# A decoder layer on one core: three more pairs of weight blocks computed with seven half products each

## The reference, cut to what matters

```python
h = x @ lw['w_in']
cq, ckv, kr, conv_in, ga, gb = jnp.split(h, IN_OFFSETS, axis=-1)
...
mix = (jax.nn.sigmoid(ga) * branch_a + jax.nn.sigmoid(gb) * branch_b) @ lw['w_out']
```

## Time and profile before

| | us |
|---|---|
| median of 3 runs (lowest to highest) | 949.93 (947.04 to 950.75) |
| the profiled execution | 949.91 |
| its span from first to last instruction | 948.2 |
| busy in the span: TensorE / VectorE / ScalarE / GpSimd | 908.6 / 466.2 / 247.4 / 96.8 |
| the chain that ended last: TensorE / DMA / VectorE | 77% / 13% / 6% |

### The profile page before, as it was taken

The page is one execution under the profiler, slowest core; times in us unless marked ns, Lnnn a source line. Parts: engine busy times, 40 slices in busy tenths (PEclk is TensorE's granted clock), DMA queues, the critical chain, the costliest instruction groups (busy, mean ns, idle before and its releaser), DMA issues.

```text
span 948.2 us, 14012 instructions
## 1 busy us (share of the span) xinstructions
PE 908.6 (96%) x5269; PEld 545.3 (58%) x5269; DVE 466.2 (49%) x1053; ACT 247.4 (26%) x540; POOL 96.8 (10%) x146
## 2 busy tenths in 40 slices
PE   8999999999999999999999999889999899897997
PEld 7777777777777766565668744443333333333444
DVE  2344477776634238777675545671111211013784
ACT  1122121122135015566640110221111111011336
POOL 0111211211211200000000000011211111111000
PEclk9999999999999999999999999999999999899999
DMA  9866898989797811011043297549999999998501
GB/s 377 351 244 244 317 331 285 306 312 344 272 357 260 288 40 54 28 40 42 10 183 153 86 429 310 203 134 394 421 424 423 423 424 424 424 417 351 229 24 66
DMA packets 65419, 247.53 MB, mean 261 GB/s; under 512 B 11301, under 2 KB 12078, under 8 KB 56358
## 3 DMA queue, kind: packets, MB, share of 16 engines
q1 hardware_dynamic: 46742, 191.41, 51.8%
q0 software_dynamic: 13216, 35.28, 10.2%
q10 hardware_dynamic: 5392, 19.93, 5.5%
HBM read 240.98 MB, written 18.05 MB: 273 GB/s over the span
## 4 chain that ended last, share of the span: by engine, by line
PE 77%; DMA 13%; DVE 6%; ACT 2%; issue 2%; SPq 1%; DVEq 0%; ACTq 0%; POOLq 0%
PE ps L1019 16%; DMA arena<-in_wexp 10%; PE ps L1512 9%; PE ps L1432 6%; PE ps L1356 4%; PE ps L1534 4%; PE ps L963 4%; PE ps L1107 3%; PE ps L1078 3%; PE ps L1192 3%; PE ps L1010 3%; PE ps L1637 2%; PE ps L1216 2%; PE ps L1156 2%; PE ps L1173 2%
## 5 line engine op out<-in xcount | busy, mean ns | idle before, releaser
L1019 PE MATMUL ps<-arena 128*128 128x260 f32 x736 | 170.7, 387 | 1.4 <-DMA arena<-in_xT 1.0
L1019 PEld LDWEIGHTS ps<-arena 128*128 128x128 f32 x736 | 137.5, 191 | 29.7 <-issue 7.5
L2043 DVE SCALAR_TENSOR_TENSOR arena<-arena,vec 128x512 f32<-128x512 f32 x120 | 81.8, 744 | 0.0
L2852 POOL DMA_DIRECT2D arena<-in_kv x96 | 51.7, 540 | 259.9 <-issue 255.4
L1512 PE MATMUL ps<-arena 128*64 128x512 f32 x288 | 66.0, 612 | 7.7 <-DMA arena<-in_wexp 6.6
L2677 DVE TENSOR_TENSOR arena<-ps,arena 128x256 f32<-128x256 f32 x18 | 7.6, 424 | 130.5 <-ACT arena L1893 130.5
L1512 PE MATMUL ps<-arena,con 128*64 128x512 f32 x288 | 65.6, 608 | 4.6 <-DMA arena<-in_wexp 4.6
L1534 PE MATMUL ps<-arena 128*64 128x512 f32 x288 | 66.8, 606 | 3.4 <-DMA arena<-in_wexp 3.4
L1432 PE MATMUL ps<-arena 128*128 128x512 f32 x128 | 58.0, 600 | 0.0
L1534 PEld LDWEIGHTS ps<-arena 128*64 128x64 f32 x288 | 21.8, 140 | 45.7 <-issue 45.7
L1512 PEld LDWEIGHTS ps<-arena 128*64 128x64 f32 x288 | 21.6, 141 | 45.9 <-issue 44.6
(11 more groups left out here) (402 smaller groups left out, 1292.6 us busy)
## 6 DMA issues: line engine op xcount, KB each, us to landing
arena<-in_wexp SPq DMA_DIRECT2D x26, 2048.0 KB, 27.1
arena<-in_kv SPq DMA_DIRECT2D x160, 272.0 KB, 9.1
arena<-in_wexp SPq DMA_DIRECT2D x36, 1024.0 KB, 27.2
arena<-in_kv POOLq DMA_DIRECT2D x96, 272.0 KB, 7.4
arena<-in_w ACTq DMA_DIRECT2D x35, 512.0 KB, 7.8
arena<-in_wexp SPq DMA_DIRECT2D x16, 512.0 KB, 9.0
arena<-in_wo SPq DMA_DIRECT2D x8, 512.0 KB, 4.2
arena<-in_w_out SPq DMA_DIRECT2D x4, 1024.0 KB, 7.4
```

Source lines behind the costliest of these rows:

```text
L1019: y = mm(ps[:, b + h, 0:TH], w[:, k], xT[:, k, h * TH:(h + 1) * TH], start=(k == 0), stop=(k == KD - 1))
L2043: y = v.scalar_tensor_tensor(out=aT[:, c, 0:NPR], in0=win, scalar=wt, in1=aT[:, c, 0:NPR], op0=ALU.mult, op1=ALU.add)
L2852: pool.dma_start(rec[:, n % 2, SPN + j], a["kv"][bass.ds(pg, 1)].rearrange("a p n -> (a p) n")).then_inc(s_kvp[n % 2], 16)
```

## The change

Gate blocks `gb` 2 to 7 (units 18 to 23) become three more pairs, numbers 3 to 5, with seven half products each. `gate_tokens` makes the token sums for them again, in the memory where `mix` is written later, since the convolution has by then overwritten the first ones; it stands in VectorE's program behind the last block of the convolution. The outputs of a pair, and the copy of `m1`, now go straight to their place in `hT` or `sigB` (`half_out`), without the scratch tiles `m1p` and `u2p`. The squares of the kv latent (`sqkv`) and the weight sums of pair 4 lie in gate blocks that are not yet written. The weight sums of pair 3 stand ahead of the reciprocal in unit `gb` 1. The sigmoid of gate blocks 0 to 3 waits for the last `c12` of pair 3, that of 4 to 7 for that of pair 5. The numbers of taps for each half unit change (`TAPS_LESS`), and since a pair counts 28 calls where two units counted 32, the places of some steps move: the program has 530 calls instead of 542, `k_step` 4 goes from unit `ks` into the second half of `gb` 0, `k_step` 5 to 7 lie behind the first half unit of pairs 3, 4 and 5, the turns behind their second and the `v_step`s behind their third; further on some steps move by one half unit. The banks' parity follows (`banks_of`, `paired_bank`).

The diff, cut:

```diff
...
-PAIRED = [5, 7, 9]
+AT = {u: i for i, u in enumerate(UNITS)}
+GROUPS = [5, AT["gb", 2]]
+PAIRS_OF = 3
+PAIRED = [i0 + 2 * n for i0 in GROUPS for n in range(PAIRS_OF)]
...
-    return 2 * ((NU - 1 - i + (i < PAIRED[0])) % 2)
+    return 2 * ((NU - 1 - i + sum(i < i0 for i0 in GROUPS)) % 2)
...
-TAPS_LESS = {("ks", 0): 0.4, ("gb", 1): 0.3, ("gb", 2): 0.5, ("kv", 0): 0.0}
+TAPS_LESS = {("ks", 0): 0.2, ("gb", 0): 0.7, ("gb", 1): 0.1, ("kv", 0): 0.0, **{("gb", j): 0.6 for j in range(2, 8)}}
...
+def goes_on(p):
+    return (p + 1) % PAIRS_OF > 0
...
+    if i == PAIRS_OF:
+        SUMS += ["t1g", "t2g", "t3g", "t4g", "t4h", f"s1p.{i}", f"s2p.{i}", f"s3p.{i}"]
...
+SUMS_PLACE = [0, 1, 0, 0, 2, 0]
+SUMS_READ = {2: 0, 3: 2, 5: 3}
...
-A_SP = [A_OLAT, A_TMP]
-A_M1P, A_U2P, A_U3P = A_QR + P, A_QR + P + TH, A_TMP + 2 * T
-assert A_U2P + TH <= A_OT and A_T4P + KD // 2 * TH <= A_TMP and A_U3P + TH <= A_R5 and B_CKV == 0
+A_SP = [A_OLAT, A_TMP, A_SIGB + 6 * T]
+A_SQKV = A_SIGB + 2 * T
+A_U3P = A_TMP + 2 * T
+A_EXW = A_U3P + TH
+A_T1G, A_T4G, A_T3G, A_T2G = A_SQ, A_SQ + 2 * T, A_SQ + 3 * T, A_SQ + 5 * T
+A_T4H = A_T2G + KD // 2 * TH
...
+        def half_out(i, x, h):
+            kind, j = UNITS[FIRST_OF[i]]
+            return (hTh if kind == "a" else sigBh)[:, j + x, h]
...
+                    if kind == "gb":
+                        act.wait_ge(s_gl, 2 * KC)
+                    av(half_out(i, 0, 0), ps[:, paired_bank(p, 0), 0:TH], ACT.Copy).then_inc(s_m1, 1)
...
+                    if at_j == 0:
+                        act.wait_ge(s_ua, TAKEN_ACT[AT["gb", 1]])
+                        act.wait_ge(s_bt, SUM[f"c12p.{PAIRS_OF}"])
+                    else:
+                        act.wait_ge(s_bt, SUM[f"c12p.{PAIRS_OF + 2}"])
...
+                if p in SUMS_READ:
+                    dve.wait_ge(s_pu, paired_product(SUMS_READ[p], "m3"))
+                if p == PAIRS_OF + 1:
+                    dve.wait_ge(s_gl, 2 * KC)
...
                 if half == 0:
                     m6 = out("m6")
                     dve.wait_ge(s_m1, p + 1)
+                    if p == PAIRS_OF:
+                        dve.wait_ge(s_gl, 2 * KC)
+                    v.tensor_tensor(c12, m6, c11, ALU.add).then_inc(s_bt, 1)
+                    wa, s2 = w1[:, weights_of(i0) % 4], s2p[sums_at(p)]
+                    v.tensor_tensor(s2, wa[:, 4:8], s2, ALU.subtract).then_inc(s_bt, 1)
+                elif half == 1:
+                    m2 = out("m2")
+                    dve.wait_ge(s_bt, SUM[f"u2p.{p}"])
+                    v.tensor_tensor(c11, m2, c11, ALU.add).then_inc(s_bt, 1)
+                    m7 = out("m7")
                     if p > 0:
-                        dve.wait_ge(s_bt, SUM[f"c12p.{p - 1}"])
-                    v.tensor_tensor(u2p, m6, m1p, ALU.add).then_inc(s_bt, 1)
-                    wa = w1[:, weights_of(i0) % 4]
-                    v.tensor_tensor(s2p[p % 2], wa[:, 4:8], s2p[p % 2], ALU.subtract).then_inc(s_bt, 1)
-                elif half == 1:
-                    v.tensor_tensor(hTh[:, j, 0], out("m2"), m1p, ALU.add).then_inc(s_bt, 1)
-                    m7 = out("m7")
-                    dve.wait_ge(s_bt, SUM[f"u2p.{p}"])
-                    v.tensor_tensor(u3p, m7, u2p, ALU.add).then_inc(s_bt, 1)
+                        dve.wait_ge(s_bt, SUM[f"c21p.{p - 1}"])
+                    v.tensor_tensor(u3p, m7, c12, ALU.add).then_inc(s_bt, 1)
                 elif half == 2:
                     m5 = out("m5")
-                    v.tensor_tensor(hTh[:, j, 1], m5, u2p, ALU.add).then_inc(s_bt, 1)
                     dve.wait_ge(s_bt, SUM[f"u3p.{p}"])
-                    v.tensor_tensor(hTh[:, j + 1, 1], m5, u3p, ALU.add).then_inc(s_bt, 1)
-                    v.tensor_tensor(hTh[:, j + 1, 0], out("m4"), u3p, ALU.add).then_inc(s_bt, 1)
-                    if p + 1 < len(PAIRED):
+                    v.tensor_tensor(c12, m5, c12, ALU.add).then_inc(s_bt, 1)
+                    v.tensor_tensor(c22, m5, u3p, ALU.add).then_inc(s_bt, 1)
+                    v.tensor_tensor(c21, out("m4"), u3p, ALU.add).then_inc(s_bt, 1)
+                    if goes_on(p):
                         paired_sums(p + 1)
                 else:
                     m3 = out("m3")
                     dve.wait_ge(s_bt, SUM[f"u4p.{p}"])
-                    v.tensor_tensor(hTh[:, j, 1], m3, hTh[:, j, 1], ALU.add).then_inc(s_bt, 1)
-                    if p + 1 < len(PAIRED):
+                    v.tensor_tensor(c12, m3, c12, ALU.add).then_inc(s_bt, 1)
+                    if goes_on(p):
                         paired_difference(p + 1)
+            def gate_tokens():
+                v.tensor_tensor(t1g, xT[:, 0:4, TH:T], xT[:, 0:4, 0:TH], ALU.subtract).then_inc(s_bt, 1)
+                dve.wait_ge(s_bt, SUM["t1g"])
+                v.tensor_tensor(t2g, xT[:, 4:8, TH:T], t1g, ALU.subtract).then_inc(s_bt, 1)
+                v.tensor_tensor(t3g, xT[:, 4:8, TH:T], xT[:, 0:4, TH:T], ALU.subtract).then_inc(s_bt, 1)
+                dve.wait_ge(s_bt, SUM["t2g"])
+                v.tensor_tensor(t4g[0], xT[:, 4:6, 0:TH], t2g[:, 0:2], ALU.subtract).then_inc(s_bt, 1)
+                v.tensor_tensor(t4g[1], xT[:, 6:8, 0:TH], t2g[:, 2:4], ALU.subtract).then_inc(s_bt, 1)
...
-                    v.tensor_tensor(sq[:, KQ:KQ + KKV], h, h, ALU.mult).then_inc(s_sq, 1)
+                    dve.wait_ge(s_gl, 2 * KC)
+                    v.tensor_tensor(sqkv, h, h, ALU.mult).then_inc(s_sq, 1)
...
                 if (kind, j) == ("gb", 1):
+                    paired_sums(PAIRS_OF)
+                    paired_difference(PAIRS_OF)
                     dve.wait_ge(s_ua, TAKEN_ACT[i - 1])
                     v.reciprocal(tmp[:, 1], tmp[:, 1]).then_inc(s_nrm, 1)
...
+                if (kind, j) == ("a", B_CB + 3):
+                    gate_tokens()
...
```

More of the change, by code:

```diff
@@ L102, in by_sum @@
 def by_sum(i):
-    return i in FIRST_OF and UNITS[i][1] < B_CB
+    return i in FIRST_OF and (UNITS[i][0] == "gb" or UNITS[i][1] < B_CB)
 TAKEN_ACT = [sum(not by_dve(m) and not by_sum(m) for m in range(i + 1)) for i in range(NU)]
@@ L183, with paired_bank, sums_at @@
 READ = {"m6": "u2", "m2": "c11", "m7": "u3", "m5": "c22", "m4": "c21", "m3": "c12"}
-def paired_bank(g):
-    return (banks_of(PAIRED[0] - 2) + g) % 4
+def paired_bank(p, n):
+    return (banks_of(GROUPS[p // PAIRS_OF] - 2) + len(PRODUCTS) * (p % PAIRS_OF) + n) % 4
+SUMS_PLACE = [0, 1, 0, 0, 2, 0]
+SUMS_READ = {2: 0, 3: 2, 5: 3}
+def sums_at(p):
+    return SUMS_PLACE[p]
 def paired_product(p, name):
@@ L283 @@
 A_T1P, A_T2P, A_T3P, A_T4P = A_EXT, A_HT, A_ACC, A_ACC + KD // 2 * TH
-A_SP = [A_OLAT, A_TMP]
-A_M1P, A_U2P, A_U3P = A_QR + P, A_QR + P + TH, A_TMP + 2 * T
-assert A_U2P + TH <= A_OT and A_T4P + KD // 2 * TH <= A_TMP and A_U3P + TH <= A_R5 and B_CKV == 0
+A_SP = [A_OLAT, A_TMP, A_SIGB + 6 * T]
[4 more added lines that the diff above has]
+A_T4H = A_T2G + KD // 2 * TH
+assert A_T4P + KD // 2 * TH <= A_TMP and A_EXW + NS * CW <= A_R5 and B_CKV == 0 and A_T4H + T <= A_OT and KQ == 3
 A_TS = A_X1
@@ L365, in decoder_layer @@
         tmph = at(A_TMP, 3 * T).rearrange("p (c h t) -> p c h t", c=3, h=2)
-        sq = at(A_SQ, 5 * T).rearrange("p (c t) -> p c t", c=5)
-        exw = at(A_TMP, NS * CW)
+        sq = at(A_SQ, KQ * T).rearrange("p (c t) -> p c t", c=KQ)
+        sqkv = at(A_SQKV, KKV * T).rearrange("p (c t) -> p c t", c=KKV)
+        exw = at(A_EXW, NS * CW)
         rcos, rsin, rsg = at(A_RQ, T), at(A_RC, T), at(A_RS, T)
@@ L427, in decoder_layer @@
         s2p = [at(off + D // 2, D // 2).rearrange("p (k m) -> p k m", k=KD // 2) for off in A_SP]
-        m1p, u2p, u3p = at(A_M1P, TH), at(A_U2P, TH), at(A_U3P, TH)
+        u3p = at(A_U3P, TH)
+        t1g, t3g, t2g = [at(off, KD // 2 * TH).rearrange("p (k t) -> p k t", k=KD // 2) for off in (A_T1G, A_T3G, A_T2G)]
+        t4g = [at(off, T).rearrange("p (k t) -> p k t", k=2) for off in (A_T4G, A_T4H)]
+        def half_out(i, x, h):
+            kind, j = UNITS[FIRST_OF[i]]
+            return (hTh if kind == "a" else sigBh)[:, j + x, h]
         sg2 = at(A_SG2, T)
@@ L946, in paired @@
                     n = PRODUCTS.index(name)
-                    g = len(PRODUCTS) * p + n
+                    first = PAIRS_OF * (p // PAIRS_OF)
+                    g = len(PRODUCTS) * (p - first) + n
                     if name == "m1":
@@ L951, in paired @@
                     if g in (0, 2):
-                        unit_out(PAIRED[0] - 2 + g // 2)
+                        unit_out(PAIRED[first] - 2 + g // 2)
                     elif g >= 4:
                         p4, n4 = divmod(g - 4, len(PRODUCTS))
+                        p4 += first
                         if n4 == 0:
@@ L962, in paired @@
                     for k in range(KD // 2):
-                        y = mm(ps[:, paired_bank(g), 0:TH], left(k), right(k), start=(k == 0), stop=(k == KD // 2 - 1))
```

(10 more changed lines are left out.)

26 lines of the change are left out of this document (10 added, 16 removed).

## The result

| | before | after |
|---|---|---|
| median of 12 runs, us (lowest to highest) | 949.06 (947.04 to 950.75) | 944.10 (941.31 to 945.84) |
| span of the profiled execution | 948.2 | 943.5 |
| from the first product of `query_sums` to the first of prompt attention | 31.38 to 340.95: 309.57 | 31.20 to 335.63: 304.43 |

The account below looks back on a forecast made before the run. TensorE was taken to bound the stage up to 340 us. Gains of 6.2 less waits of 0.9, 0.15 and 0.3 gave 4.9 us off 949.91: 945.0 us, forecast 943.5 to 946.5, range 942.8 to 949.7.

Parts of the forecast that it names:

- The calls: TensorE's program in the stage: 12 calls, 24 records less at 0.219 us each, 5.3 us gained.
- `v_step` 4: TensorE's wait for VectorE before this step goes, as rope products no longer stand before its copy: 0.4 us gained.
- The expected 0.15 in front of `gb` 1: TensorE waits 0.15 us there, because ScalarE empties `kv` only behind the exponential of `k_step` 4.
- Step 9's pages: The score step's wait for cache pages goes, with 36 calls between request and scores instead of 32: 0.57 us gained.
- The 0.3 us that I set against it on the other side: Page waits at `k_step` 4, 10 and 15, left only 32 calls: 0 to 0.57 us each, 0.3 in all.
- Turn 7: `k_turn` 7 in pair 5 waits for a late exponential: 0.9 us taken, bounds 0.25 and 3.8, sign 0.3 to 1.5.
- the layout: TensorE's and VectorE's queues laid out from pair 3's first product; it gave `k_turn` 7 a wait of 0.5 us.
- fixed latency for each instruction: On VectorE, 21 additions and 12 sums would cost 2.8 us more, nearly 2 of it in front of `k_turn` 7.
- The first (VectorE the bound): Rival: VectorE's instructions all at full length, turns 6 and 7 wait 3.8 us instead of 0.9: 948; chance 0.18.
- The third (late blocks): Rival: weight blocks of pair 5, then of `ga` 0 and 1, land late and hold VectorE: 955 us; chance 0.08.
- The fourth (no arrival: 948 to 950): Rival: the stage ends 5 us earlier but the expert stage shifts against its own loads; chance 0.10.
- the second: Rival: cache pages late in three short intervals, GpSimd's requests perhaps slowed beside VectorE: 946.4 to 949.7 us; chance 0.12.

Follow-up runs that it names:

- Experiment 1: Kernel before with the eighth chunk of the contraction left out of gate blocks 2 to 7, 12 calls less; 944.8 us, ratio 0.9956.
- experiment 3: Changed kernel with the share of convolution taps in the half units of gate blocks 2 to 7 at 1.0 instead of 0.6; 949.35 us.
- experiment 4: Changed kernel with pair 5's two weight blocks requested behind step 6's exponential instead of behind the last `c12` of pair 3; 946.37 us.

## Why the prediction was right

**The calls.** Taken as 5.3 us. From the first product behind `v_step` 4 to the first of `ga` 0 the stage lost, step 8's scores taken off before, 209.68 - 148.40 - 2.73 = 58.55 against 201.11 - 147.65 = 53.46, which is 5.09 with turn 7's 0.16 in it: 5.25. Experiment 1 gives 5.2 by itself. The cheaper of the two record prices was the right one.

**`v_step` 4.** Taken as 0.4. It went, but not for the reason given. The rope products still stand between the step and its copy; here the first of them and the copy, in VectorE's timeline after:

```profile
139.85 0.69 DVE L2275 TENSOR_TENSOR arena<-arena 32x520 f32<-32x520 f32 x1
...
144.15 0.68 DVE L2096 COPY arena<-ps 128x512 f32<-128x512 f32 x1
```

From `peaks` to this copy VectorE takes 8.6 us, before it took 7.3. What removed the wait is that the scores come 2.9 us earlier (132.78 against 135.68 in the chain), while `v_step` 4 starts only 0.75 earlier (145.71 against 146.46 in the timelines), 0.4 of it the wait itself. Ahead of the pairs' place the two chains differ by 0.57 us (19.15 against 18.58 from the half unit in front of the step or of `kv`), 0.4 of it this wait; the rest is of the size of one switch between kinds of work (3.70 against 3.51 for 16 records). The expected 0.15 in front of `gb` 1 is not to be found as a wait.

**Step 9's pages.** This term failed. The 0.57 us were put down to the interval, as something that the change takes away for good; the second profile of the same kernel has no such wait, so it belongs to an execution and not to the interval alone. The 0.3 us that I set against it on the other side was of the same kind: 1.10 in one profile, above the 0.6 that I allowed for, and 0 in the next. The two stood on opposite sides of the sum, which hid part of the error. One profile shows that a wait can happen, not that it does.

**Turn 7.** Taken as 0.9 between bounds of 0.25 and 3.8; it was 0.16 in both profiles, below both the lower bound and the 0.3 to 1.5 that I named as its sign. The place and the cause (the sigmoid ahead of the copy of `m1`) were right. I had the layout at 0.5 and then went up from it out of caution; the layout itself was late by only 0.3 us at `u2` of pair 5, mostly since `c12` of pair 4 came 37.9 behind the start and not 38.5. The queued prices of the earlier trace rows held: three additions in a row stand 0.34 us apart in the trace after, as before. By the fixed latency for each instruction that the Trainium skill states (VectorE: DVE Perf Modes, the section on the TRN2 errata), paid in a full queue too, this turn would have waited nearly 2 us more by the prediction's estimate; the trace does not show that cost here.

**Sum.** 5.25 + 0.57 - 0.16 = 5.66, measured 5.67 in the stage without page waits. These terms are read from the same chains, so this says that nothing is left over, not that they were foreseen. The forecast had 4.9 for the stage, 0.8 less. It held 0.74 us too much waiting at turn 7 and 0.45 in two waits that did not come or that come and go; against that it counted 0.57 too much gain at step 9 and 0.17 too little ahead of pair 3. The whole run shows 5.0 (the interval reaches from 4.2 to 5.9, and 5.67 lies in it). So the mechanism was right, and that 4.9 and 5.0 agree to a tenth is in part luck.

**What follows the stage** varies: from 606.0 to 608.1 us in thirteen profiles, without any order by the length of the stage. Part of it goes with TensorE's granted clock. Behind the stage every profile has stretches at 1.2 GHz, 15 to 22 us in all: 15.2 in the profile with 606.0, 22.3 in that with 608.1, though one with 15.1 has 607.7. The times go the same way: of the 48 runs of the kernel before in the three sets, the 14 with a mean granted clock of 0.990 or less took 949.8 us on average, the 26 with 0.992 or more 948.7. No experiment changes the clock, so this is not shown as a cause.

**The rivals.** The first (VectorE the bound) was wrong for this kernel, and experiment 3 shows how near it lay: 14 taps more and the gain is gone. The third (late blocks) is real as a mechanism (experiment 4, by way of turn 7 and not of `m1`), but its margin was there: requested at 168.0, needed at 180.7. The fourth (no arrival: 948 to 950) is refuted by the run, 944.10 with at least 4.2 us of gain. Of the second, that a block shares the DMA engines with the pages is shown, that GpSimd's requests slow down beside VectorE is not: six requests take 3.5 us in fifteen of the sixteen loads and 3.8 in one, in both kernels.

**Left open:** how often each kernel waits for pages, why a load takes 17.7 or 20.7 us, and what the clock behind the stage depends on, since each profile shows one execution.

## What to carry to other kernels

Lay out the queues of the two busiest engines side by side with start-to-start prices from the trace, and look for the first instruction that is due before it can be ready; here that gave the place of every wait on an engine in the changed kernel and in experiment 3, with sizes that were up to 0.8 us too large, and one small wait that did not come. Arithmetic taken off the bounding engine pays one for one only while the engine that makes up for it has room, so shift its other work away first, as the taps were here. A wait for a DMA in a single profile is not a term of a sum: take a second profile, or bound it by nothing and by its size.

## What the runs showed that I had not expected

A wait of TensorE of 2.42 us inside a full stage was followed by some 3.4 us at half the clock (0.50 granted from 196 to 199 us) and cost 1.7 us on top of itself (experiment 4); a wait of 2.80 us in experiment 3 was not, with the clock at 1.00 in every window from 170 to 212 us. A load of 16 pages, 4.5 MB, took 17.7 to 20.7 us with the same program around it but for half a unit. And a weight block of 0.5 MB requested among the pages moved their median landing by 1.0 to 2.1 us.
